# The second four heads' probabilities turned through DRAM in a hybrid decoder layer

## The reference, cut to what matters

```python
h = rmsnorm(x, pre_mix_norm)
rq, rk, rv, rg, mq, mk, mv = split(h @ w_in)
ret  = silu(rg) * head_rmsnorm(retention(rotary(rq), rotary(rk) * 64 ** -0.5, rv))
moba = softmax(mq @ mk.T * 64 ** -0.5 + bias[t5_bucket], causal) @ mv    # 8 heads of 64, 256 keys
x = x + rmsnorm(concat([ret, moba]) @ w_out, post_mix_norm)
h = rmsnorm(x, pre_ffn_norm)
x = x + rmsnorm((silu(h @ w_gate) * (h @ w_up)) @ w_down, post_ffn_norm)
```

## Time and profile before

| | us |
|---|---|
| median of 3 runs | 299.92 |
| lowest, highest run | 299.44, 300.46 |
| profiled execution, its own time | 300.19 |
| its span in the trace | 297.5 |
| PE busy in the span | 290.9 |
| DVE busy | 190.2 |
| ACT busy | 151.8 |
| POOL busy | 12.0 |

### The profile page before, as it was taken

The page is one execution under the profiler, slowest core; times in us unless marked ns, Lnnn a source line. Parts: engine busy times, 40 slices in busy tenths (PEclk is TensorE's granted clock), DMA queues, the critical chain, the costliest instruction groups (busy, mean ns, idle before and its releaser), DMA issues.

```text
span 297.5 us, 4101 instructions
## 1 busy us (share of the span) xinstructions
PE 290.9 (98%) x1396; PEld 235.6 (79%) x1396; DVE 190.2 (64%) x287; ACT 151.8 (51%) x241; POOL 12.0 (4%) x20
## 2 busy tenths in 40 slices
PE   8999999999999999999999999999999999999992
PEld 3788877887888888888878888888888888888881
DVE  2857469995787779798393846456383836451246
ACT  4898565835482746495272725243362726231331
POOL 0030000000020013200000000000000000000001
PEclk9999999999999999999999999999999999999999
DMA  6999993958436450749879593948767694415003
GB/s 195 397 405 385 408 391 146 287 174 273 151 109 223 160 184 23 243 172 351 303 263 300 211 301 132 289 169 235 258 200 241 187 289 158 125 53 159 0 0 141
DMA packets 24744, 64.62 MB, mean 217 GB/s; under 512 B 2803, under 2 KB 8476, under 8 KB 24732
## 3 DMA queue, kind: packets, MB, share of 16 engines
q1 hardware_dynamic: 24336, 63.36, 63.2%
q0 software_dynamic: 304, 1.06, 1.0%
q10 hardware_dynamic: 92, 0.05, 0.1%
HBM read 60.25 MB, written 4.21 MB: 217 GB/s over the span
## 4 chain that ended last, share of the span: by engine, by line
PE 97%; DVE 1%; DVEq 0%; ACT 0%; issue 0%
PE bank L1042 29%; PE bank L1044 28%; PE bank L1043 28%; PE bank L1074 1%; PE bank L1090 1%; PE bank L1094 1%; PE bank L1098 1%; PE bank L1052 1%; PE bank L1158 1%; PE bank L1197 1%; PE bank L1061 1%; DVE res L1033 1%; DVE res L1027 1%; PE bank L1184 1%; PE bank L1206 0%; PE bank L1207 0%
## 5 line engine op out<-in xcount | busy, mean ns | idle before, releaser
L1042 PE MATMUL bank<-w_hi,a_hi 128*128 128x512 f32 x256 | 100.9, 394 | 0.0
L1044 PE MATMUL bank<-w_hi,a_lo 128*128 128x512 f32 x256 | 99.9, 390 | 0.0
L1043 PE MATMUL bank<-w_lo,a_hi 128*128 128x512 f32 x256 | 99.6, 389 | 0.0
L1042 PEld LDWEIGHTS bank<-w_hi,a_hi 128*128 128x128 f32 x256 | 48.1, 188 | 10.6 <-issue 0.8
L1044 PEld LDWEIGHTS bank<-w_hi,a_lo 128*128 128x128 f32 x256 | 48.0, 188 | 10.2
L1043 PEld LDWEIGHTS bank<-w_lo,a_hi 128*128 128x128 f32 x256 | 48.1, 188 | 9.8
L936 DVE TENSOR_TENSOR w_lo<-raw,w_hi 128x1024 fp32r<-128x1024 f32 x40 | 47.9, 1234 | 1.4 <-ACT w_hi L649 1.4
L740 DVE TENSOR_TENSOR w_lo<-raw,w_hi 128x1024 fp32r<-128x1024 f32 x32 | 37.9, 1220 | 12.9 <-ACT w_hi L511 12.9
L649 ACT ACTIVATE w_hi<-raw 128x1024 fp32r<-128x1024 f32 x40 | 40.3, 1052 | 3.7 <-DMA raw<-in_w_gu 3.7
L1042 PE MATMUL bank<-d_hi,h_hi 128*128 128x512 f32 x88 | 34.5, 392 | 0.0
L1043 PE MATMUL bank<-d_lo,h_hi 128*128 128x512 f32 x88 | 34.4, 390 | 0.0
(11 more groups left out here) (114 smaller groups left out, 259.3 us busy)
## 6 DMA issues: line engine op xcount, KB each, us to landing
raw<-in_w_gu SPq DMA_DIRECT2D x44, 512.0 KB, 5.0
raw<-in_w_dn SPq DMA_DIRECT2D x22, 512.0 KB, 5.0
raw<-in_w_in SPq DMA_DIRECT2D x20, 512.0 KB, 8.4
raw<-in_w_out SPq DMA_DIRECT2D x8, 512.0 KB, 4.7
h_rows<-hid_sq SPq DMA_DIRECT2D x9, 256.0 KB, 2.0
hid_T<-h_rows SPq DMA_DIRECT2D x36, 64.0 KB, 4.2
raw<-in_w_in SPq DMA_DIRECT2D x8, 256.0 KB, 5.7
xs<-in_x SPq DMA_DIRECT2D x2, 512.0 KB, 8.3
```

The source lines that it names most:

```text
L1042: pe.matmul(acc, hi, wh, start=first, stop=False)
L1043: pe.matmul(acc, hi, wl, start=False, stop=False)
L1044: return pe.matmul(acc, lo, wh, start=False, stop=last)
```

## The change

The second four heads take the way that the first four have.

- The scaling of heads 4 to 7 goes from DVE to GpSimd: DVE only takes the reciprocal and counts up `erec_ready`, GpSimd does the eight multiplications in place, and counts up `pn_ready`.
- DVE turns heads 4 to 7 in 32x32 blocks at u = 17 (`SQ_T2`), into the same view `pr_sq` of `pT`, once the first store from it is done.
- SP stores that to the same `p_rows` before the load of unit 24, once the first four heads are read back; after the load of unit 25 it waits for the store and reads back in four transfers into `pr` itself (`pT_second`), and then goes on with unit 26.
- PE's 24 turning products at u = 18 and ACT's four copies are gone. PE waits ahead of the product with v for eight transfers in place of four. It reads heads 4 to 7 through the same strided view as heads 0 to 3.

```diff
-SQ_T, FOURS_T = 13, 18
+SQ_T, SQ_T2 = 13, 17
...
+            def store_squares(rows, src, heads):
+
+                sp.wait_ge(pr_sq_ready, heads)
+                sp.dma_start(rows, src.rearrange("p q h i c -> p q (h i c)")).then_inc(pr_sq_stored, 16)
+
+            def load_turned_pr(rows, dst, batch):
+
+                sp.wait_ge(pr_sq_stored, 16 * batch)
+                row = 4 * 3 * B
+                for q in range(Q):
+                    sp.dma_start(dst[q * B:(q + 1) * B].rearrange("p q h i c -> p q (h i c)"),
+                                 bass.AP(rows.tensor, q * row, [[Q * row, B], [B * Q * row, Q], [1, row]])
+                                 ).then_inc(pT_loaded, 16)
...
             for i in range(N_OUT):
+                if i == 0:
+                    sp.wait_ge(pT_loaded, 16 * Q)
+                    store_squares(p_rows, pr_sq, MH)
+                if i == 2:
+                    load_turned_pr(p_rows, pT_second, 2)
                 load(N_IN + i, (N_IN + i) % RAW, w_out[i])
...
+            for h in range(4, MH):
+                pool.wait_ge(erec_ready, h - 3)
+                for t, (a, b) in enumerate([(0, P), (P, 3 * P)]):
+                    pool.tensor_scalar(pr[:, h % 4, a:b], pr[:, h % 4, a:b], erec[:, t, h:h + 1], None,
+                                       ALU.mult).then_inc(pn_ready, 1)
...
-                if u - 1 == FOURS_T:
-                    act.wait_ge(pr_sq_stored, 16)
-                    for h in range(4, MH):
-                        act.wait_ge(pt_done, h // 2 * 2 - 2)
-                        act.activation(pT[:, h % 4, :].rearrange("p (n f i) -> p n f i", f=2, i=H),
-                                       turned_halves(h), ACT.Copy).then_inc(pT_ready, 1)
...
-                    small(dve.reciprocal(erec[:, :, h:h + 1], esum[:, :, h:h + 1]))
+                    recip = dve.reciprocal(erec[:, :, h:h + 1], esum[:, :, h:h + 1])
+                    if h >= 4:
+                        recip.then_inc(erec_ready, 1)
+                        continue
+                    small(recip)
...
-                for h in range(4) if u == SQ_T else ():
+                if u == SQ_T2:
+                    dve.wait_ge(pr_sq_stored, 16)
+                for h in range(4) if u == SQ_T else range(4, MH) if u == SQ_T2 else ():
                     dve.wait_ge(pn_ready, NT * (h + 1))
...
-                if u == FOURS_T:
-                    pe.wait_ge(l_ready, MH)
-                    for h in range(4, MH):
-                        pe.wait_ge(pn_ready, NT * (h + 1))
-                        for i in range(3):
-                            ins = turn_halves(turned_halves(h)[:, i, :, :], pr[:, h % 4, i * P:(i + 1) * P])
-                        ins.then_inc(pt_done, 1)
...
-                    pe.wait_ge(pT_loaded, 16 * Q)
+                    pe.wait_ge(pT_loaded, 2 * 16 * Q)
```

More of the change, by code:

```diff
@@ L231, in hybrid_layer @@
         pT_loaded = sem("pT_loaded")
-        pt_done = sem("pt_done")
-        pT_ready = sem("pT_ready")
+        erec_ready = sem("erec_ready")
         pv_done = sem("pv_done")
@@ L295, in hybrid_layer @@
         pr_sq = pT[:, :, :].rearrange("p h c -> p (h c)").rearrange("p (q h i c) -> p q h i c", q=Q, h=4, i=3)
+        pT_second = pr[:, :, :].rearrange("p h c -> p (h c)").rearrange("p (q h i c) -> p q h i c", q=Q, h=4, i=3)
         def probabilities(h, t):
[L298 to L304, removed]
+            src = pT_first if h < 4 else pT_second
+            return src[:, :, h % 4, 2 * t:2 + t, :].rearrange("p q i c -> p i q c")
         def retention_bank(h):
@@ L396, in _ @@
                 if n == SQ_T + LEAD + 4:
-                    sp.wait_ge(pr_sq_ready, 4)
-                    sp.dma_start(p_rows, pr_sq.rearrange("p q h i c -> p q (h i c)")).then_inc(pr_sq_stored, 16)
+                    store_squares(p_rows, pr_sq, 4)
                 if n == SQ_T + LEAD + 6:
[L400 to L405, removed]
+                    load_turned_pr(p_rows, pT_first, 1)
                 if n == 12:
@@ L418, in _, with store_hidden @@
                 load(base + s, (base + s) % RAW, w_gu[s])
-            def store_squares(g):
+            def store_hidden(g):
                 sp.wait_ge(sq_ready, NT * g)
@@ L438, in group @@
                 if not (isinstance(g, int) and g <= 2):
-                    store_squares(g - 2)
+                    store_hidden(g - 2)
                 for j in range(DN):
@@ L451, in _ @@
                 group(g + 1, gu_n(4, 0))
-            store_squares(NF - 2)
+            store_hidden(NF - 2)
             for j in range(DN):
@@ L824, in _ @@
                     rotary(1)
-                for h in range(4) if u == SQ_T else ():
+                if u == SQ_T2:
+                    dve.wait_ge(pr_sq_stored, 16)
+                for h in range(4) if u == SQ_T else range(4, MH) if u == SQ_T2 else ():
                     dve.wait_ge(pn_ready, NT * (h + 1))
-                    dve.transpose(pr_sq[:, :, h, :, :].rearrange("p q i c -> p i q c"),
-                                  pr[:, h, :].rearrange("p (i q c) -> p i q c", i=3, q=Q)).then_inc(pr_sq_ready, 1)
+                    dve.transpose(pr_sq[:, :, h % 4, :, :].rearrange("p q i c -> p i q c"),
+                                  pr[:, h % 4, :].rearrange("p (i q c) -> p i q c", i=3, q=Q)).then_inc(pr_sq_ready, 1)
                 if u <= RS_U:
@@ L1177, in _ @@
                     pe.wait_ge(rT_ready, NT)
-                    pe.wait_ge(pT_ready, 4)
                     pe.wait_ge(rv_nat, NT)
```

## The result

| | before | changed |
|---|---|---|
| median, us | 299.68 (4 runs) | 304.65 (4 runs) |
| lowest, highest | 299.00, 300.46 | 302.40, 306.72 |
| profiled execution: time, span | 300.19, 297.5 | 304.79, 303.0 |

The ratio is 1.0163, with a 95% interval from 1.0135 to 1.0190: the change costs 4.9 us. The forecast was 302.3 us, 2.4 us over before, with a range up to 304.4. The sign was right, the size half of what was measured. The same kernel was run again beside the experiments and gave 302.85 us (4 runs, ratio 1.0123, interval 1.0074 to 1.0172). So its own level is uncertain by 2 us, and that spread turns out to be part of the answer.

The account below looks back on a forecast made before the run. PE's own work, busy 98% of the span, was taken as the bound. The 2.4 us later product with v, with 0.79 us already subtracted, on the median of 299.92 gave 302.3 us, range 300.6 to 304.4.

Parts of the forecast that it names:

- That PE's wait ahead of the product with v would decide, and nothing else: PE stands in line 1197's wait from 71.7 to 74.3; the product with v starts 2.4 us later than before.
- What PE is rid of, 0.79 us: The 24 turning products between 63.30 and 64.09 leave PE's own chain: 0.79 us less; nothing else leaves PE.
- DVE wins only 0.5 us of its eight multiplications: On DVE, only what stood between the reciprocal of head 7 (ended 56.63) and rotary (57.13) is won: 0.5 us.
- GpSimd takes 4 to 5 us and is hidden: GpSimd's multiplications of heads 4 to 7 end at about 59.3, 1.9 us before DVE wants them; lateness had chance 0.12.
- a sign of being wrong: GpSimd's multiplications reaching past 61 us, so that DVE's turning waits for them, would show the forecast wrong.
- the two bounds of 3.9 and 9.2 us: GpSimd's four heads: 3.9 us by columns alone, 9.2 us with 0.67 us on top for each of eight instructions.
- Contention on DVE, 0.3 us: In rotary, DVE's two-input addition (line 780) is held up by GpSimd's multiplication: 0.3 us, bounds 0 and 1.1 us.
- PE waits 0.6 us for `w_lo` of unit 19: At unit 19 PE wants `w_lo` at 63.90, DVE ends it at 64.5: a wait of 0.6 us.
- The way through DRAM, 10.8 us from store to last landing: Second store at 63.5, last read landed at 74.3: 10.8 us, as before; transfers in time or partly faster had 0.15.
- The company is the same: In both round trips two 512 KB loads stand right behind the store and further loads behind the reads.
- PE's clock would not fall, 0.02: PE idles 2.6 us at 71.7 ahead of the product with v; no clock fall expected, the rival having 0.02.
- The late `w_out` loads at nothing: Loads of units 26 to 31, delayed behind the reads, cost nothing; up to 2 us if ACT's idle cover were gone.

Follow-up runs that it names:

- the kernel with the split wait: Changed kernel, but PE waits for the first four transfers ahead of heads 0 to 3, the second four only ahead of heads 4 to 7: 300.08 us, ratio 1.0039.
- the reads alone: Changed kernel, but SP issues the second reads right behind the second store and the w_out loads only when they have landed: 305.79 us, one run.
- the two such held kernels: Changed kernel, but SP holds the loads of units 26 and on until the second reads have landed, run twice: 302.18 and 301.89 us.
- the filled wait: Changed kernel, but PE makes 14 products of constants ahead of its wait for the second reads: 302.83 us, ratio 1.0092.
- the product behind unit 21: Changed kernel, but PE makes the product with v after unit 21 and two retention heads, its result split at u = 22: 299.39 us, ratio 0.9986.

## Why the prediction was half right

**That PE's wait ahead of the product with v would decide, and nothing else:** right. Without that wait the kernel is at 0.9972 of before, and with PE's order changed the loss is gone.

**What PE is rid of, 0.79 us:** right as far as can be seen: with 0.32 us of the new wait at unit 19 in it, the run without the wait for the reads gained 0.8 us (0.4 to 1.3 by the interval).

**DVE wins only 0.5 us of its eight multiplications:** right (5.25 against 4.75 us).

**GpSimd takes 4 to 5 us and is hidden:** the size was wrong, 6.47 us; the verdict right, with far less cover than thought. It was done at 61.24, past the 61 us that the prediction had named as a sign of being wrong, but DVE turned only from 61.37. The forecast had 1.9 us to spare. Undisturbed, 128 columns took some 600 ns and 256 columns some 915, which puts the sum between the two bounds of 3.9 and 9.2 us.

**Contention on DVE, 0.3 us:** too much; the two additions took 0.71 and 0.77 us against 0.69, 0.1 us together. It was GpSimd that stood: its multiplication of 256 columns that started at 58.3, beside DVE's addition at 58.26, took 1.44 us in place of 0.92. DVE's second addition, at 60.57, began while GpSimd's last multiplication ran (60.3 to 61.24), and lost 0.08 us; it was not held until that was over, as the subtraction at 115.26 was the earlier trace rows.

**PE waits 0.6 us for `w_lo` of unit 19:** 0.34 us.

**The way through DRAM, 10.8 us from store to last landing:** this step failed. The term that was mis-sized is the last read, 5.4 us from issue to landing; it took 6.64 us in the first profile and 5.43 in the second, so that the whole way took 12.1 and 10.8 us. "The company is the same" was not: behind the first reads stood one load, since the load after it waited for `w_lo` of unit 19 (its row gives only the 22 us for all eight); behind the second stood five, three of them issued from 69.35 within 1 us, since DVE had the `w_lo` ready that they wait for. By the table above that alone costs nothing, in the two traces that show it. With a 16 KB instruction packet in the same stretch it costs 1.1 to 1.5 us. In none of the traces did such a packet fall on the first four heads' reads, so the row that the forecast took could not show it.

**PE's clock would not fall, 0.02:** this step failed too, and cost as much. It was put at nothing from a stretch of 4 us without a fall, cut off at 296. The same trace has the fall in its next us, 4.4 us after PE's last product ended; and in the trace of the kernel with the split wait, whose last product ended at 294.5, the clock was low 2.1 us later (stretches as above, the first of the kernel before):

```profile
296.00:297.00 1.00, 0.00 (x0) 0.00 (x0) 0.00 (x0) 0.00 (x0) 0.00 (x0) 0.58 0.57 223
...
294.60:296.60 2.00, 0.00 (x0) 0.00 (x0) 1.90 (x5) 0.67 (x2) 0.55 (x1) 1.00 0.70 262
296.70:300.00 3.30, 0.00 (x0) 0.00 (x0) 1.05 (x2) 0.00 (x0) 0.00 (x0) 0.50 0.42 159
```

At the end of the 14 traces the clock falls 2.1 to 4.9 us after PE's last product, so for a wait of 2.6 us, which was the forecast's own, a fall could not be put at nothing. After the waits of 3.9 us it fell in both profiles that had one, and after the 3.3 us at the end of the section on the reads alone. After waits of 2.6 us it did not in three profiles; among the executions of the two such held kernels 3 of 13 have a mean clock as low as the runs with a fall, but how long PE stood in those three is not recorded. In the run that kept PE at work it never did.

**The two together:** the product with v started at 75.65 in place of the forecast's 74.3 and took 1.57 us more: 302.3 + 1.35 + 1.57 = 305.2, against 304.79 for the profiled execution and 304.65 for the median. The trial with the filled wait keeps the first failed term and takes away the second: 302.83 us. All six executions of the changed kernel above 302.3 have a mean clock of 0.992 or less, which points to the clock for what they have above 302.8; but the 306.72 of the slowest is 3.9 us above it, more than the 2.6 us of the dearest fall that a trace shows, and the rest stays open. The forecast's 302.3 is also what the changed kernel comes near to when neither happens (301.34 and 301.60), and that depends on when the packet falls, not on anything that the prediction had worked out.

**The late `w_out` loads at nothing:** right for the changed kernel (ACT's idle time ahead of line 613 is still 4.91 us). The trial with the reads alone, which has unit 24's load another 8.3 us later, shows what stood behind that cover: 3.3 us of PE, where the forecast had up to 2 us. It also named the wrong reader: the first to wait was not the output projection, but the retention scores that stand behind `w_lo` of unit 24 in DVE's list.

## What to carry to other kernels

The first round trip landed 11 us before its reader came; the second was started 8.3 us before it and takes 11 to 12. Count back from the reader first, and put other work of the bounding engine between, as the product behind unit 21 did. When a wait appears on TensorE, price it twice, the wait itself and a stretch at half clock behind it, unless a row shows a wait of that very length without a fall several times over. Before a row is used to say that something does not happen, read the stretch right behind it: here the fall stood one us further on. And when the time of a DMA is taken from an earlier one like it, look at all that shares its time, the transfers issued behind it and the packets of other queues, and at more than one execution.

## What the runs showed of the hardware that was not expected

- A single instruction packet of 16 KB made the last of four reads of 192 KB land 1.1 to 1.5 us later (6.5 to 6.9 us against 5.4) when loads of 512 KB stood right behind it: six of six profiles with both, and neither of the two with the loads but no packet. With the packet and no loads it was 0.3 us, in one profile. The first of the four reads landed after 3.9 to 4.2 us in all six.
- The clock fell 2.1 to 4.9 us after PE's last product in the 14 traces, and in the middle of a trace after waits of 3.9 us (twice) and 3.3 us (once), there only when PE was at work again. Three waits of 2.6 us passed without. Falls cost 1.6 and 2.6 us in two traces. With the packet this makes the same program spread over 5 us (301.34 to 306.72 in eight executions), where it spreads over 1.2 us once PE does not stand.
- GpSimd's multiplication with one tensor input takes some 915 ns for 256 columns and 600 for 128: 2.5 ns for each further column on top of some 0.3 us. Its addition with two inputs takes 1289 ns for 512 columns, less than the 1.5 us that this line would give, so a second input costs it nothing that shows.
